# VectorE adds each gated block to x itself, and GpSimd has no part in the products

## The reference

```python
sh1, sc1, g1, sh2, sc2, g2 = split(silu(c) @ w_mod + b_mod, 6)   # one set for latent, one for context tokens
# layers 0 and 1                                   # layers 2 and 3
x = x + g1 * (mixer(norm(x) modulated) @ w_o)      # x = LN(ALPHA * x + g1 * (mixer(x modulated) @ w_o))
x = x + g2 * mlp(norm(x) modulated)                # x = LN(ALPHA * x + g2 * mlp(x modulated))
mlp = lambda h: square(relu(h @ w1)) @ w2          # 1024 -> 4096 -> 1024
```

## Time and profile before

| what | value |
|---|---|
| median of 3 runs | 3666.88 us (3666.8 to 3667.98) |
| the profiled execution: its time | 3667.81 us |
| the profiled execution: its span | 3666.0 us |
| TensorE, VectorE, ScalarE, GpSimd busy | 96%, 59%, 36%, 22% |
| GpSimd's adds (L594) | 360, 493.4 us in all |
| VectorE's gates (L586) | 360, 244.9 us in all |

### The profile page before, as it was taken

How to read it: one execution, slowest core, us unless ns; L and a number is a source line. 1 busy time by engine, 2 the same in 40 slices (tenths; PEclk the granted TensorE clock), 3 DMA queues, 4 the chain that set the end, 5 groups by cost and what they waited for, 6 DMA issues and landing times. The chain is left out here.

```text
span 3666.0 us, 51840 instructions
## 1 busy us (share of the span) xinstructions
PE 3523.4 (96%) x19275; PEld 2904.9 (79%) x19275; DVE 2158.5 (59%) x3180; ACT 1338.1 (36%) x2349; POOL 819.8 (22%) x600
## 2 busy tenths in 40 slices
PE   6999999999999999999999999999989989899998
PEld 4877788888878787777778888888878866678886
DVE  5748756565564464444458485665666638855445
ACT  3338641221243563222348332212233335523222
POOL 1510013213223111222120121231200019712222
PEclk9999999999999999999999999999999989999999
DMA  5224123333322204444210123323221230133231
GB/s 194 70 86 145 66 84 121 109 105 107 119 65 69 84 30 150 160 154 155 75 58 2 47 103 120 109 103 109 92 69 57 93 118 21 38 104 104 92 103 69
DMA packets 164783, 344.40 MB, mean 94 GB/s; under 512 B 8732, under 2 KB 18429, under 8 KB 164605
## 3 DMA queue, kind: packets, MB, share of 16 engines
q1 hardware_dynamic: 160493, 332.98, 26.7%
q10 hardware_dynamic: 4144, 9.44, 0.7%
HBM read 333.75 MB, written 12.85 MB: 95 GB/s over the span
## 5 line engine op out<-in xcount | busy, mean ns | idle before, releaser
L594 POOL TENSOR_TENSOR x<-x,scaled_buf 128x512 f32<-128x512 f32 (+1 forms) x360 | 493.4, 1386 | 2073.1 <-DVE scaled_buf L586 2072.4
L132 DVE TENSOR_TENSOR w_lo<-raw,w_hi 128x2048 fp32r<-128x2048 f32 x198 | 465.6, 2352 | 675.1 <-ACT w_hi L126 665.8
L126 ACT ACTIVATE w_hi<-raw 128x2048 fp32r<-128x2048 f32 x197 | 377.4, 1916 | 1281.8 <-PE psum L407 1279.4
L405 PE MATMUL psum<-hT_hi,w_hi 128*128 128x512 f32 (+1 forms) x1888 | 668.7, 354 | 3.2 <-DVE hT_lo L881 2.4
L406 PE MATMUL psum<-hT_lo,w_hi 128*128 128x512 f32 (+1 forms) x1888 | 665.2, 352 | 0.0
L407 PE MATMUL psum<-hT_hi,w_lo 128*128 128x512 f32 (+1 forms) x1888 | 664.6, 352 | 0.0
L405 PE MATMUL psum<-w_hi,uT_hi 128*128 128x512 f32 x1280 | 503.1, 393 | 0.0
L407 PE MATMUL psum<-w_hi,uT_lo 128*128 128x512 f32 x1280 | 498.6, 390 | 0.0
L406 PE MATMUL psum<-w_lo,uT_hi 128*128 128x512 f32 x1280 | 498.2, 389 | 0.0
L586 DVE TENSOR_TENSOR scaled_buf<-psum,gate 128x512 f32<-128x512 f32 x360 | 244.9, 688 | 328.2 <-PE psum L407 285.2
L405 PE MATMUL psum<-w_hi,hT_hi 128*128 128x512 f32 x1072 | 420.4, 392 | 3.3 <-issue 3.3
(11 more groups left out here) (307 smaller groups left out, 4583.2 us busy)
## 6 DMA issues: line engine op xcount, KB each, us to landing
raw<-in_w_mlp SPq DMA_DIRECT2D x64, 1024.0 KB, 5.3
raw<-in_ff_w SPq DMA_DIRECT2D x64, 1024.0 KB, 5.1
mod_wide<-in_w_mod SPq DMA_DIRECT2D x32, 1536.0 KB, 8.4
mod_wide<-in_w_mod SPq DMA_DIRECT2D x8, 3072.0 KB, 10.5
raw<-in_ssm_w_in SPq DMA_DIRECT2D x20, 1024.0 KB, 5.1
mod_slab<-in_w_mod SPq DMA_DIRECT2D x8, 2048.0 KB, 8.4
raw<-in_a_w_qkv SPq DMA_DIRECT2D x12, 1024.0 KB, 5.0
raw<-in_b_w_qkv SPq DMA_DIRECT2D x12, 1024.0 KB, 5.0
```

Source lines behind the costliest of these rows:

```text
L126: act.activation(K.w_hi[h][:, :, :], K.raw[h][:, :, :], ACT.Copy).then_inc(K.hi_done.h, 1)
L132: dve.tensor_tensor(K.w_lo[h][:, :, :], K.raw[h][:, :, :], K.w_hi[h][:, :, :].bitcast(F32), ALU.subtract).then_inc(K.lo_done.h, 1)
L405: pe.matmul(out, hi_a, hi_w, start=first, stop=False, **check)
L594: pool.tensor_tensor(x, x, K.scaled_buf[:, j % 2, :], ALU.add).then_inc(K.added.h, 1)
```

## The change

GpSimd's add moves to VectorE, right behind the gate, in `gate_out`; VectorE waits for its own gate before it. GpSimd's blocks are taken out of both stages, and what they waited for at their start (K.small_loaded and K.gained in a projection, K.gained in an MLP) VectorE waits for, ahead of its loop. In layer 3's projection, where VectorE itself does the affine steps, it waits for the count ahead of them.

```diff
@@ gemm_stage
+    gained = affine.ga0 if affine is not None else K.gained.n
...
             if evac_on == "dve":
+                dve.wait_ge(K.small_loaded.h, K.small_loaded.n)
+                dve.wait_ge(K.gained.h, gained)
                 dve.wait_ge(K.gate_done.h, K.gate_done.n)
             ahead_loop(dve, st, body)
...
-        if evac_on == "dve":
-            @block.gpsimd
-            def _(pool):
-                blocks = stream.count // per
-                pool.wait_ge(K.small_loaded.h, K.small_loaded.n)
-                pool.wait_ge(K.gained.h, K.gained.n)
-                with pool.Fori(0, blocks) as n:
-                    for j, t in enumerate(tiles):
-                        residual_add(K, pool, K.scaled.n + nt * n + j, t, n, j)
@@ gate_out
     dve.tensor_tensor(K.scaled_buf[:, j % 2, :], bank[:, :], K.gate[:, cls, ds(n * SLAB_N, SLAB_N)], ALU.mult)\
        .then_inc(K.scaled.h, 1)
-
-
-def residual_add(K, pool, count, t, n, j):
-
-    pool.wait_ge(K.scaled.h, count + 1)
+    dve.wait_ge(K.scaled.h, count + 1)
     x = K.x[:, t, ds(n * SLAB_N, SLAB_N)]
-    pool.tensor_tensor(x, x, K.scaled_buf[:, j % 2, :], ALU.add).then_inc(K.added.h, 1)
+    dve.tensor_tensor(x, x, K.scaled_buf[:, j % 2, :], ALU.add).then_inc(K.added.h, 1)
@@ mlp_stage
+            dve.wait_ge(K.gained.h, K.gained.n)
             dve.wait_ge(K.gate_done.h, K.gate_done.n)
...
-        @block.gpsimd
-        def _(pool):
-            pool.wait_ge(K.gained.h, K.gained.n)
-            with pool.Fori(0, chunks) as c:
-                for h in range(2):
-                    for j, t in enumerate(tiles):
-                        residual_add(K, pool, sc0 + 2 * nt * c + h * nt + j, t, h, j)
```

## The result

The changed kernel takes 3685.89 us (median of 3 runs, 3685.8 to 3686.64) against 3666.88: 1.0053 of the time before, 95% interval 1.0040 to 1.0067. The forecast was 3683.4, range 3673 to 3694. A second set of runs on another chip gave 3687.6 against 3666.4 there, ratio 1.0058 (1.0041 to 1.0075). The profiled execution took 3685.8, its span is 3684.0.

A forecast was written before the change was run, and what follows sets the result against it. TensorE, busy 96%, was taken to bound the kernel, losing time only where it waits. Terms 5.6 + 1.8 + 6.1 + 1.4 + 0.8 + 1.0 + 2.5 - 2.7 = +16.5 us gave 3683.4, range 3673 to 3694.

The forecast's parts named there:

- the moved wait: Layer 3's projection: VectorE waits for the row loads before the first w_lo, which TensorE needs; +2.5 us, bounds 0 to 4.
- The pair: On VectorE, a gate with its add takes 0.72 + 0.61 = 1.33 us; bounds 1.22 to 1.58.
- The turns: MLPs of layers 0 and 2: TensorE's second turn waits for mod_sum, 0.4 us in 14 chunks; +5.6 us.
- Layer 2's last chunk: Layer 2's MLP: VectorE hardly idles in its last chunk, so all twelve adds lie on the path; +6.1 us.
- rival 1: Not slower: VectorE's adds hide in its idle 41% and quicker normalises pay the rest; 3664.2 us, 5%.
- Layer 2's projection: At its end tiles take 3.05 us on VectorE against 2.72 from TensorE; three lags and the last add, +1.4 us.
- The gains: Ends without layer norm: -0.9 us in layer 0's and layer 1's projections, -0.6 and -0.3 in layer 1's and 0's MLPs.
- I leave that to the range: Longer TensorE idles can cost 1 to 2 us more at the lower clock; not in the sum.
- Layer 3's projection end: Four tiles with layer norm, one lag, by the same steps as layer 2's projection; +0.8 us.
- The waits on gained: VectorE's new waits on gained are for its own work and cost a step.
- (3): Rival: a waited step on VectorE costs 0.28 us, so each turn comes 1.75 us later; 3715 us, 7%.
- (4): Rival: chunks and row loads cost nothing and the long end half; 3670.5 us, no change to be told, 3%.

The follow-up runs named there:

- two-and-two kernel: The changed kernel with the adds of the first column half (layers 0 and 2) in twos: gate, gate, add, add; 3677.88 us, ratio 1.0032.
- the halves: VectorE adds only in the four projections (3672.94 us) or only in the four MLPs (3679.29 us), GpSimd elsewhere as in the kernel before.
- three-stage kernel: VectorE adds only in the projections of layers 0 and 1 and in layer 1's MLP, GpSimd elsewhere; 3662.93 us, ratio 0.9988 to the kernel before.
- last experiments: The changed kernel and the kernel before run once more, unaltered: 3687.6 us (4 runs) and 3663.59 us (one run).
- the wait alone: The kernel before with only VectorE's wait for the row loads added ahead of the projections; 3671.53 us, ratio 1.0017.
- the MLPs alone: VectorE adds in the four MLPs, GpSimd in the projections as in the kernel before; 3679.29 us, ratio 1.0032.

## Why the prediction was right

It was right in direction, in the mechanism at nearly every place and, but for the moved wait, in size; the likeliest case came true. The forecast change was +16.5; the medians give +19.0 in the first set and +21.2 in the second, the places +20.6 and +20.9.

- **The pair.** 1.33 forecast, 1.33 seen; the two-and-two kernel shows that 0.11 to 0.13 of it is the wait on the instruction just ahead.
- **The turns.** Cover gone by 0.35 to 0.44 forecast; 0.37 to 0.45 lost in thirteen of the fourteen chunks, some 0.3 in layer 0's last, whose turn shows no wait. Moving only the sum clears it, so the order on VectorE's queue and not its load is the cause.
- **Layer 2's last chunk.** The end forecast at +6.1 came at +5.93 behind the first gate, +6.0 to +6.4 at its place (up to 0.7 of it clock, as the halves show), and the normalises took 0.81 as forecast. The relief from GpSimd's absence is real and far too small for rival 1.
- **Layer 2's projection.** The last normalise ends at 2122.87, 2.19 later; 0.75 of that had been lost earlier by the marks of the first two profiles, so +1.44 against +1.4. Another 0.4 us passes between it and the first hT cast (2.60 instead of 2.15). It goes with the clock: TensorE's transposes in between (L261) have a granted clock of 0.50 from their start at 2123.02, while before the first 1.25 us of them, from 2120.83, went at 1.00.
- **The gains** came in the forecast direction (forecast -0.9, -0.9 and -0.6), as the three-stage kernel shows by itself. Only the first is clean, -0.85 to -0.86; the other two are -0.4 to -1.3 and -0.3 to -0.7, by the clock of the profiles compared.
- **The moved wait is the term that was mis-sized**: +2.5, bounds 0 to 4; it measured 4.7 to 6.1. The mechanism was right, and the idle time nearly so, 2.9 to 3.4 us (the rows landed 7.5 us behind their last issue; 6.8 was worked out). What failed is "I leave that to the range": the lower clock behind a long idle was seen in the earlier trace rows and kept out of the sum. With it the place took 3.6 us more than forecast in the first profile of the changed kernel, more than the whole 2.5 from 3683.4 to 3685.9, and 2.4 more in the second, half of the 4.7 by which the second set's change goes beyond +16.5.
- **Layer 3's projection end** is +0.8 in three profiles (this kernel's first among them) and +2.3 or +2.4 in five. The five have the stretch at the lower clock at the start of the MLP (last experiments), the three don't. Three kernels with GpSimd's adds in this projection (the wait alone, the MLPs alone, the three stages) have the same granted clock here as the three, 0.87 and then 1.00, and stand at 0.0. So the adds cost the +0.8 that was forecast, and the rest is clock; what puts the later stretch there is open.
- **The waits on gained** were put at a step. One shows 0.35 us of idle on VectorE ahead of layer 2's MLP; at its place the changed kernel loses 0.41 or 0.42, but a kernel without that wait (the wait for rows alone) loses 0.36 there too, so nothing can be told.
- **The other rivals.** 0.28 for a wait (3) is excluded by the pair; no chunk, row load or end was free as in (1) and (4).

## What to carry to other kernels

An engine's idle share says nothing of its order: VectorE was idle 41% of the span, and the change still costs some 20 us, because sums and normalises that TensorE needs stood behind the adds in its queue, and a w_lo behind the wait that moved with them. Look at what stands behind the added instruction, put the work that another engine waits for ahead of it, and move only the adds that gain: here those of the three stages that end with neither layer norm nor modulation sums. When TensorE comes to stand idle for about 3 us, price the slower matmuls behind the gap as well as the gap. And before a difference of 1 or 2 us at one place is put down to a change, compare the granted clock there in both profiles.

## What the runs showed of the hardware that was not expected

The price of the clock: behind an idle of 2.9 to 3.4 us the granted clock was 0.50 for about 3 us in six profiles and for 6 in one, 1.6 to 1.9 or 3.1 us lost; 26 transposes in the gap kept it at 1.00. Such stretches come and go between profiles of one kernel: the same 198 us of an untouched stage took 1.6 to 4.4 us longer in the nine profiles of fourteen that had one. And an instruction that waits for the one just ahead on VectorE costs 0.12 to 0.13 us, so a row of dependent pairs is 10% shorter when two pairs are interlaced.
